# Gate and up products of 18 features as seven half-size block products

## The chip, the core and the metric

One core of a Trainium2 chip runs the whole program. The metric is the time of one execution in device microseconds (us), the median of several runs. The engines are TensorE (PE in the profile; its weight loads PEld), VectorE (DVE), ScalarE (ACT), GpSimd (POOL) and SyncE (SP, which issues the DMAs). Each works through its own instructions in program order and waits on counting semaphores.

## The reference

Two layers on 512 tokens of width 1024, float32, each with a feed-forward (FFN), a token mixer, and a second feed-forward; then a last norm.

```python
def swiglu(h, w_gate, w_up, w_down):
    return (jax.nn.silu(h @ w_gate) * (h @ w_up)) @ w_down

for l in range(DEPTH):                      # DEPTH = 2, D_MODEL = 1024, D_FF = 2816, SEQ = 512
    x = x + 0.5 * swiglu(rmsnorm(x, ffn1_norm[l]), ffn1_w_gate[l], ffn1_w_up[l], ffn1_w_down[l])
    ...                                     # x = x + [ssd || hgrn2](rmsnorm(x) @ w_in[l]) @ w_out[l]
    x = x + 0.5 * swiglu(rmsnorm(x, ffn2_norm[l]), ffn2_w_gate[l], ffn2_w_up[l], ffn2_w_down[l])
return rmsnorm(x, final_norm)
```

The change touches the four feed-forwards only; the mixers stay as they are.

## The kernel before

Everything lies with channels on the 128 partitions and the 512 tokens along the free side. x is 8 tiles of 128x512 that stay in SBUF. A float32 product is made of three matmuls of type float32r: each operand is split in a high part (a copy rounded to float32r, by ScalarE) and a low part (operand minus high part), and `products` adds high x high, high x low and low x high in PSUM (lines 1467 to 1469).

Weights come in **blocks** of 128x1024 floats (eight 128x128 tiles). There are four buffers each for the raw block (`raw`), its high part (`whi`) and its low part (`wlo`), and block w uses buffer w mod 4. For every block SyncE issues a DMA when the low part of block w-4 is made (`split`), ScalarE copies raw to `whi` when the products of block w-4 are done (`blk`; `hi`, `hi_i`), and GpSimd subtracts to make `wlo` (L481, semaphore `high` to `split`). TensorE waits for `split`.

A feed-forward (`ffn(c, wb, ...)` exists once for each engine; c is 0 or 1) has 44 gate and up blocks, two for each of 22 features of 128 (a "feature" here is a tile of 128 hidden units, gate block first). The first four blocks are interleaved (`up_staggered`: steps 0 to 10, block q takes the input tile k = step - q), since the input tiles `hhi`, `hlo` arrive one by one. The norm's factor per token is not in them: TensorE turns the sums of squares (`norm_turns`, after step 6), VectorE makes the reciprocal root, TensorE spreads it (`norm_spreads`, after step 8), and VectorE keeps it in `r`. Each gate and up product leaves PSUM through VectorE times `r` (L962, L964). Then ScalarE applies silu (L551), VectorE multiplies (L967), ScalarE copies the high part to `ahi` (L555), and VectorE makes the low part `alo` (L969). `ahi` and `alo` hold all 22 features.

The down product follows: for each of the 8 output tiles m, 22 x 3 matmuls over three blocks, and VectorE adds half of it to x (L985); ScalarE and VectorE make the next stage's `hhi` and `hlo` (L506, L848) and the sum of squares (L498, L858).

The order of the work is the order in which these functions are written, one program for each engine; there is no scheduler.

## Time and profile before

| | us |
|---|---|
| median of 3 runs | 1927.21 (1926.32 to 1927.46) |
| span of the profiled execution | 1927.2 |
| TensorE busy | 1919.3 |
| VectorE, ScalarE, GpSimd busy | 754.3, 701.8, 904.0 |

A row of a group of instructions gives line, engine, operation, output<-inputs, shape and count, then the busy time, the mean of one in ns, and the idle time of the engine just before them with what ended it. Matmuls overlap, so their spacing (from start to start) tells what one costs, not the duration in the row.

### The profile page before, as it was taken

To read this page: it belongs to the slowest core of one execution; us is meant where nothing else is said; L and a number is where in the kernel's file an instruction comes from. 1 tells how busy PE (TensorE), PEld (TensorE's weight loads), DVE (VectorE), ACT (ScalarE), POOL (GpSimd) and SP (SyncE) were. 2 spreads that over 40 slices of the span, in tenths; PEclk is the share of its full clock that TensorE was granted. 3 is DMA by queue.
4 is the path that set the end of the run, shared out by engine and by line. 5 is a ranking of instruction groups with operands and counts; after the bars stand their busy time and mean duration, and the time that the engine had idled before them with its cause. 6 is when DMAs were issued, how large, how long until landed. Compare 5 with 4: busy or idle time off the path is not lost.

```text
span 1927.2 us, 28344 instructions
## 1 busy us (share of the span) xinstructions
PE 1919.3 (100%) x10396; PEld 1579.1 (82%) x10396; DVE 754.3 (39%) x1209; ACT 701.8 (36%) x975; POOL 904.0 (47%) x550
## 2 busy tenths in 40 slices
PE   9999999999999999999999999999999999999999
PEld 7888888788788888888888888887878888888887
DVE  6222221389875322231132222214898752222312
ACT  5222222365643322222332222324556432222223
POOL 3444444466335544444444444444654444444443
PEclk9999999999999999999999999999999999999999
DMA  5332333322213333333323333332222223333332
GB/s 182 104 99 90 96 97 99 99 67 89 67 55 99 109 98 98 97 90 100 103 93 98 99 91 93 97 100 89 78 79 75 66 91 108 98 98 95 91 100 97
DMA packets 53504, 181.84 MB, mean 94 GB/s; under 512 B 6816, under 2 KB 6816, under 8 KB 53408
## 3 DMA queue, kind: packets, MB, share of 16 engines
q1 hardware_dynamic: 53264, 180.56, 30.1%
q8 instruction: 60, 0.98, 0.2%
q14 instruction: 36, 0.29, 0.1%
q10 hardware_dynamic: 144, 0.00, 0.0%
HBM read 178.45 MB, written 2.10 MB: 94 GB/s over the span
## 4 chain that ended last, share of the span: by engine, by line
PE 99%; DMA 0%; ACT 0%; DVE 0%; issue 0%; SPq 0%; ACTq 0%
PE ps L1467 31%; PE ps L1469 31%; PE ps L1468 31%; PE ps L1685 1%; PE ps L1602 1%; PE ps L1604 1%; PE ps L1603 1%; PE ps L1733 0%; PE ps L1799 0%; PE ps L1963 0%; PE ps L1746 0%; PE ps L1804 0%; DMA x<-in_x 0%; PE ps L1487 0%; PE ps L1783 0%; PE ps L1717 0%
## 5 line engine op out<-in xcount | busy, mean ns | idle before, releaser
L481 POOL TENSOR_TENSOR wlo<-raw,whi 128x1024 fp32r<-128x1024 f32 (+1 forms) x536 | 901.7, 1698 | 1015.2 <-ACT whi L542 553.6
L1467 PE MATMUL ps<-hhi,whi 128*128 128x512 f32 x1760 | 691.6, 393 | 2.2 <-DVE hlo L848 1.7
L1469 PE MATMUL ps<-hhi,wlo 128*128 128x512 f32 x1760 | 686.5, 390 | 0.0
L1468 PE MATMUL ps<-hlo,whi 128*128 128x512 f32 x1760 | 686.3, 390 | 0.0
L1467 PEld LDWEIGHTS ps<-hhi,whi 128*128 128x128 f32 x1760 | 330.9, 188 | 76.1 <-issue 4.1
L1469 PEld LDWEIGHTS ps<-hhi,wlo 128*128 128x128 f32 x1760 | 330.9, 188 | 69.6
L1468 PEld LDWEIGHTS ps<-hlo,whi 128*128 128x128 f32 x1760 | 331.0, 188 | 67.4
L1469 PE MATMUL ps<-ahi,wlo 128*128 128x512 f32 x704 | 274.1, 389 | 0.0
L1467 PE MATMUL ps<-ahi,whi 128*128 128x512 f32 x704 | 274.1, 389 | 0.0
L1468 PE MATMUL ps<-alo,whi 128*128 128x512 f32 x704 | 274.1, 389 | 0.0
L536 ACT ACTIVATE whi<-raw 128x1024 fp32r<-128x1024 f32 x168 | 177.2, 1055 | 265.3 <-PE ps L1469 246.0
L964 DVE TENSOR_TENSOR u<-ps,r 128x512 f32<-128x512 f32 x88 | 60.8, 691 | 368.5 <-PE ps L1469 368.5
L542 ACT ACTIVATE whi<-raw 128x1024 fp32r<-128x1024 f32 x176 | 183.5, 1045 | 38.9 <-PE ps L1469 38.9
L555 ACT ACTIVATE ahi<-u 128x512 f32 (+1 forms) x88 | 55.6, 632 | 389.1 <-DVE u L967 389.1
L985 DVE SCALAR_TENSOR_TENSOR x<-ps,x 128x512 f32<-128x512 f32 x32 | 22.1, 692 | 368.7 <-PE ps L1469 368.7
L1467 PEld LDWEIGHTS ps<-ahi,whi 128*128 128x128 f32 x704 | 132.2, 188 | 27.5
L1468 PEld LDWEIGHTS ps<-alo,whi 128*128 128x128 f32 x704 | 132.2, 188 | 27.4
L1469 PEld LDWEIGHTS ps<-ahi,wlo 128*128 128x128 f32 x704 | 132.2, 188 | 27.2
L551 ACT ACTIVATE g<-g 128x512 f32<-128x512 f32 x88 | 55.6, 631 | 237.9 <-DVE g L962 237.9
L962 DVE TENSOR_TENSOR g<-ps,r 128x512 f32<-128x512 f32 x88 | 60.8, 691 | 167.6 <-PE ps L1469 166.7
L969 DVE TENSOR_TENSOR alo<-u,ahi 128x512 f32 x88 | 66.1, 751 | 81.7 <-ACT ahi L555 81.7
L506 ACT ACTIVATE hhi<-x,par 128x512 fp32r<-128x512 f32 x48 | 34.6, 721 | 152.5 <-DVE x L985 132.8
(276 smaller groups left out, 1354.6 us busy)
## 6 DMA issues: line engine op xcount, KB each, us to landing
raw<-in_up SPq DMA_DIRECT2D x168, 512.0 KB, 3.4
raw<-in_mix SPq DMA_DIRECT2D x64, 512.0 KB, 3.4
raw<-in_dn SPq DMA_DIRECT2D x64, 448.0 KB, 3.3
raw<-in_dn SPq DMA_DIRECT2D x32, 512.0 KB, 3.5
raw<-in_lead SPq DMA_DIRECT2D x8, 512.0 KB, 3.5
x<-in_x SPq DMA_DIRECT2D x8, 256.0 KB, 6.2
raw<-in_lead SPq DMA_DIRECT2D x8, 256.0 KB, 6.3
raw<-in_mix SPq DMA_DIRECT2D x8, 256.0 KB, 2.5
```

The costliest lines, as they stand in the source:

```text
L481: low = pool.tensor_tensor(wlo[:, q, part], raw[:, q, part], whi[:, q, part].bitcast(F32), ALU.subtract)
L506: act.activation(hhi[:, m, :], x[:, m, :], ACT.Copy, scale=gain).then_inc(x_high.sem, 1)
L536: act.activation(whi[:, q, :], raw[:, q, :], ACT.Copy).then_inc(high.sem, 1)
L542: act.activation(whi[:, q, :], raw[:, q, :], ACT.Copy).then_inc(high.sem, 1)
L551: act.activation(g2[:, jj, :], g2[:, jj, :], ACT.Silu).then_inc(silu_g.sem, 1)
L555: act.activation(ahi[:, 2 * i + jj, :], u2[:, jj, :], ACT.Copy).then_inc(hid_high.sem, 1)
L962: made(g_out, tt(g2[:, jj, :], bank(jj), r[:], ALU.mult))
L964: made(u_out, tt(u2[:, jj, :], bank(2 + jj), r[:], ALU.mult))
L969: made(hid_low, tt(alo[:, 2 * i + jj, :], u2[:, jj, :], ahi[:, 2 * i + jj, :].bitcast(F32), ALU.subtract))
L1467: mm(dst, whi[:, q, s], mh, start=start, stop=False)
L1468: mm(dst, whi[:, q, s], ml, start=False, stop=False)
L1469: return mm(dst, wlo[:, q, s], mh, start=False, stop=stop)
```

## The change

It applies to features 4 to 21 of each feed-forward; features 0 to 3 (`PLAIN`) stay as before. Such a feature is a **unit**. Its two blocks, gate and up, are each cut in the halves k = 0 to 3 and 4 to 7 of the input channels: A11, A12 (gate) and A21, A22 (up), each 128x512. The tokens are cut in two halves of 256 (`HT`). The seven products of Strassen's scheme in Winograd's form are A11 B11, S1 T1, S2 T2, S4 B22, S3 T3, A12 B21 and A22 T4, each of 4 x 3 matmuls with 256 columns (`half_product`). The weight sums S1 = A21 + A22, S2 = S1 - A11, S4 = A12 - S2 are made by VectorE in PSUM (`make_sum`), S3 = A11 - A21 by GpSimd in SBUF (`make_s3`). ScalarE copies the high part of each of the seven to a slot of `whi` (`slot_hi`), and the low parts are made by VectorE (the three sums, `slot_low`) and GpSimd (A11, S3, A12, A22).

The token side has seven terms for each of four channel pairs k, 7 x 256 = 1792 columns: B11, B21, B22 and T1 to T4. `make_terms(k)` (VectorE) makes them from x, the norm's gain and `r`, so the norm is already in them; ScalarE copies the high part (`terms_hi`), and the low part is made by VectorE for k = 0, 1 and by GpSimd for k = 2, 3 (`terms_low`). All four must be there before the first unit.

Partial results are summed in PSUM as far as the scheme lets them; ScalarE copies three intermediate banks to SBUF (`copy_first`, `copy_second`, `copy_third`), VectorE adds them (`gate_second`, `up_second`, `gate_first`). A unit is finished before the next one ends its own products.

The features are worked in two parts, 0 to 11 and 12 to 21, each followed by a down product over its features (two blocks for each of 8 output tiles); the first adds to x at once (`x_part`). So the hidden tiles need less room, and the terms get it. From the second feed-forward on, the norm's turn and spread stand after steps 3 and 5 of the interleaved blocks; in the very first they stay after 6 and 8. All loops over features are now written out.

```diff
@@ -34,8 +34,43 @@
-DN_PIECES = [(0, 8), (8, 15), (15, 22)]
-DN_BLOCKS = KD * len(DN_PIECES)
+
+
+PLAIN = 4
+UNITS = NJ - PLAIN
+PARTS = [(0, 12), (12, NJ)]
+PIECES = [[(0, 6), (6, 12)], [(12, 17), (17, 22)]]
+HT = T // 2
+KH = KD // 2
+HW = KH * P
+
+
+T1, T3, T2, T4, B21, B22, B11, B12 = range(8)
+TERMS = 7
+MOVES = (B11, T1, T2, B22, T3, B21, T4)
+A11, S1, S2, S4, S3, A12, A22 = range(7)
+
...
+        def slot(weights, i):
+
+            return weights[:, i // 2, i % 2 * HW:i % 2 * HW + HW]
+
+        def quarter(b, k):
+
+            return raw[:, b % NS, k * HW:k * HW + HW]
+
...
+                def terms_low(k):
+                    pool.wait_ge(terms_high.sem, terms_high.upto(l, KH * c + k))
+                    pool.tensor_tensor(tlo[c][:, k, :], terms[c][k % 2][:, 0:TERMS, :].rearrange("p i t -> p (i t)"),
+                                       thi[c][:, k, :].bitcast(F32), ALU.subtract).then_inc(terms_low_pool.sem, 1)
...
+                def prepare(u):
+                    low_a11(u)
+                    make_s3(u)
+                    low_s3(u)
+                    low_a12(u)
+
+                for b in range(NS, 2 * PLAIN):
+                    low(l, wb + b)
+                    if b >= 2 * PLAIN - 2:
+                        terms_low(b - 2 * PLAIN + KH)
+                for part, (j0, j1) in enumerate(PARTS):
+                    u0 = max(j0, PLAIN)
+                    prepare(u0)
+                    for u in range(u0, j1):
+                        low_a22(u)
+                        if u + 1 < j1:
+                            prepare(u + 1)
+                    for m in range(KD):
+                        for i, (k0, k1) in enumerate(PIECES[part]):
+                            low(l, wb + down_block(part, m, i), (k1 - k0) * P)
...
+                    def terms_hi(k):
+                        act.wait_ge(terms_made.sem, terms_made.upto(l, KH * c + k))
+                        act.activation(thi[c][:, k, :], terms[c][k % 2][:, 0:TERMS, :].rearrange("p i t -> p (i t)"),
+                                       ACT.Copy).then_inc(terms_high.sem, 1)
...
+                    terms_hi(0)
+                    hi(wb + 4)
+                    plain_silu(0)
+                    hi(wb + 5)
+                    terms_hi(1)
+                    plain_silu(1)
+                    hi(wb + 6)
+                    hi(wb + 7)
+                    hidden_hi(0)
+                    terms_hi(2)
+                    hidden_hi(1)
+                    terms_hi(3)
+                    plain_silu(2)
+                    slot_hi(PLAIN, A11)
+                    hidden_hi(2)
+                    slot_hi(PLAIN, S1)
+                    slot_hi(PLAIN, S2)
+                    slot_hi(PLAIN, S4)
+                    plain_silu(3)
+                    slot_hi(PLAIN, S3)
+                    slot_hi(PLAIN, A12)
+                    hidden_hi(3)
...
+                    def make_terms(k):
+                        t = terms[c][k % 2]
+                        if k >= 2:
+                            ready(terms_low_dve, 2 * c + k - 2)
+                        did(stt(t[:, B21:B22 + 1, :].rearrange("p i t -> p (i t)"), x[:, KH + k, :], gain(KH + k), r[:],
+                                ALU.mult, ALU.mult))
+                        did(stt(t[:, B11:B12 + 1, :].rearrange("p i t -> p (i t)"), x[:, k, :], gain(k), r[:],
+                                ALU.mult, ALU.mult))
+                        settle()
+                        did(tt(t[:, T1, :], t[:, B12, :], t[:, B11, :], ALU.subtract))
+                        did(tt(t[:, T3, :], t[:, B22, :], t[:, B12, :], ALU.subtract))
+                        settle()
+                        did(tt(t[:, T2, :], t[:, B22, :], t[:, T1, :], ALU.subtract))
+                        settle()
+                        made(terms_made, tt(t[:, T4, :], t[:, B21, :], t[:, T2, :], ALU.subtract))
+
+                    def terms_low(k):
+                        ready(terms_high, KH * c + k)
+                        made(terms_low_dve, tt(tlo[c][:, k, :],
+                                               terms[c][k % 2][:, 0:TERMS, :].rearrange("p i t -> p (i t)"),
+                                               thi[c][:, k, :].bitcast(F32), ALU.subtract))
...
+                    def make_sum(u, n):
+
+                        b, v = wb + up_block(u), index(u)
+                        dst = bank(sum_bank(u, n))
+                        if n == 2 or u > PLAIN:
+                            ready(slot_low_dve, 3 * v + n - 2)
+                        if u == PARTS[1][0] + 1 and n == 0:
+                            ready(x_part, KD * c + KD - 1)
+                        if n == 0:
+                            loaded_block(b + 1)
+                            ins = tt(dst, quarter(b + 1, 0), quarter(b + 1, 1), ALU.add)
+                        elif n == 1:
+                            loaded_block(b)
+                            ready(sum_made, 3 * v)
+                            ins = tt(dst, bank(sum_bank(u, 0)), quarter(b, 0), ALU.subtract)
+                        else:
+                            ready(sum_made, 3 * v + 1)
+                            ins = tt(dst, quarter(b, 1), bank(sum_bank(u, 1)), ALU.subtract)
+                        made(sum_made, ins)
+
+                    def slot_low(u, n):
+                        i = (S1, S2, S4)[n]
+                        ready(slot_high, 5 * index(u) + i)
+                        made(slot_low_dve, tt(slot(wlo, i), bank(sum_bank(u, n)), slot(whi, i).bitcast(F32),
+                                              ALU.subtract))
...
+                    def up_second(u):
+                        ready(unit_done, 5 * index(u) + S3)
+                        ready(unit_copied, 3 * index(u) + 1)
+                        made(unit_out, tt(upper(u)[1][:, HT:T], bank(unit_banks(u)[0])[:, 0:HT], sq[:, HT:T], ALU.add))
+
...
+                    for part, (j0, j1) in enumerate(PARTS):
+                        u0 = max(j0, PLAIN)
+                        for u in range(u0, j1):
+                            more = u + 1 < j1
+                            if u > u0:
+                                hidden_first(u - 1)
+                            if more:
+                                make_sum(u + 1, 0)
+                                make_sum(u + 1, 1)
+                            if u > u0:
+                                hidden_lo(u - 1)
+                            if more:
+                                slot_low(u + 1, 0)
+                                make_sum(u + 1, 2)
+                                slot_low(u + 1, 1)
+                            gate_second(u)
+                            if more:
+                                slot_low(u + 1, 2)
+                            up_second(u)
+                            gate_first(u)
+                            hidden_second(u)
+                        hidden_first(j1 - 1)
+                        hidden_lo(j1 - 1)
+                        if part == 0:
+                            u = PARTS[1][0]
...
+                        return products(bank(2 * (q % 2) + q // 2), q, k, h_tile(k, c), k == 0, k == KD - 1)
+
+                    turns_at, spreads_at = (KD - 2, KD) if (l, c) == (0, 0) else (3, 5)
...
+                    def half_product(u, i, dst, start):
+
+                        cols = slice(MOVES[i] * HT, MOVES[i] * HT + HT)
+                        wh, wl = slot(whi, i), slot(wlo, i)
+                        for k in range(KH):
+                            s = slice(k * P, k * P + P)
+                            mm(bank(dst)[:, 0:HT], wh[:, s], thi[c][:, k, cols], start=start and k == 0, stop=False,
+                               skip_group_check=True)
+                            mm(bank(dst)[:, 0:HT], wh[:, s], tlo[c][:, k, cols], start=False, stop=False,
+                               skip_group_check=True)
+                            last = mm(bank(dst)[:, 0:HT], wl[:, s], thi[c][:, k, cols], start=False, stop=k == KH - 1,
+                                      skip_group_check=True)
+                        last.then_inc((unit_done if i < A12 else blk).sem, 1)
+
+                    def unit(u):
+
+                        q, z, y = unit_banks(u)
+                        v, b = index(u), wb + up_block(u)
+                        ready(slot_low_pool, 2 * v)
+                        if u == PLAIN:
+                            ready(terms_low_dve, 2 * c + 1)
+                            ready(terms_low_pool, 2 * c + 1)
+                        if u < PLAIN + 2:
+                            ready(g_out, PLAIN * c + PLAIN - 1)
+                            ready(u_out, PLAIN * c + PLAIN - 1)
+                        else:
+                            ready(hid, NJ * c + u - 2)
+                        half_product(u, A11, q, True)
+                        ready(slot_low_dve, 3 * v)
+                        if u >= PLAIN + 2:
+                            ready(unit_out, 3 * (v - 2))
+                        half_product(u, S1, z, True)
+                        ready(slot_low_dve, 3 * v + 1)
+                        ready(unit_copied, 3 * v)
+                        half_product(u, S2, q, False)
+                        ready(slot_low_dve, 3 * v + 2)
+                        ready(unit_copied, 3 * v + 1)
+                        half_product(u, S4, z, False)
+                        ready(slot_low_pool, 2 * v + 1)
+                        ready(unit_copied, 3 * v + 2)
+                        half_product(u, S3, q, False)
+                        ready(split, b)
+                        if u >= PLAIN + 2:
+                            ready(unit_out, 3 * (v - 2) + 2)
+                        half_product(u, A12, y, True)
+                        ready(split, b + 1)
+                        ready(unit_out, 3 * v + 1)
+                        half_product(u, A22, q, False)
+
```

**First place: ScalarE at the start of a feed-forward.** Before, with `whi<-raw` the copies of weight blocks, `g<-g` the silu:

```order
L541 ISA [waits raw_full0]
L542 ACT_TABLE_LOAD
L542 ACTIVATE whi<-raw 128x1024 [waits blk]
L550 ISA
L551 ACT_TABLE_LOAD
L551 ACTIVATE g<-g 128x512 [waits g_out]
```

and now, with `thi` the high part of the terms:

```order
L720 ACTIVATE thi_65<-terms_0_61 128x1792 [waits terms_made]
L705 ISA
L711 ISA [waits raw_full0]
L712 ACTIVATE whi<-raw 128x1024 [waits blk]
L727 REGISTER_ALU
L724 ACT_TABLE_LOAD
L724 ACTIVATE g<-g 128x512 [waits g_out]
```

The copy of block 4 stood first and needed only its data; now the high part of terms(0), which needs `r`, stands ahead of it.

**Second place: GpSimd in the first feed-forward's plain phase.** Before, with one subtraction for each weight block:

```order
L481 TENSOR_TENSOR wlo<-raw,whi 128x1024 [waits high]
L478 REGISTER_ALU
L481 TENSOR_TENSOR wlo<-raw,whi 128x1024 [waits high]
L478 REGISTER_ALU
L481 TENSOR_TENSOR wlo<-raw,whi 128x1024 [waits high]
```

and now, from block 5 on (block 4's stands ahead of these):

```order
L586 TENSOR_TENSOR wlo<-raw,whi 128x1024 [waits high] x2
L595 TENSOR_TENSOR tlo_67<-terms_0_61,thi_65 128x1792 [waits terms_high]
L586 TENSOR_TENSOR wlo<-raw,whi 128x1024 [waits high]
L595 TENSOR_TENSOR tlo_67<-terms_1_62,thi_65 128x1792 [waits terms_high]
L599 TENSOR_TENSOR wlo<-raw,whi 128x512 [waits slot_high]
L612 TENSOR_TENSOR s_69<-raw 128x512 [waits raw_full1,raw_full0]
```

Two term lows of 1792 columns (`tlo`) have moved in, the first between the weight blocks 6 and 7, the second behind block 7; then come the first unit's A11 and S3.

**Third place: VectorE in a feature.** Before, one of the two features of the loop's body:

```order
L962 TENSOR_TENSOR g<-ps,r 128x512 [waits blk]
L963 ISA
L964 TENSOR_TENSOR u<-ps,r 128x512 [waits blk]
L965 ISA
L966 ISA [waits u_out]
L967 TENSOR_TENSOR u<-g,u 128x512 [waits silu_g]
L969 ISA [waits hid_high]
L969 TENSOR_TENSOR alo<-u,ahi 128x512
```

and now, from the middle of a steady unit u (`wlo<-ps,whi` is a slot low of unit u+1, `ps<-raw,ps` its third sum, the 256-column rows gate_second, up_second and gate_first of unit u):

```order
L1338 TENSOR_TENSOR wlo<-ps,whi 128x512 [waits slot_high]
L1233 REGISTER_ALU [waits slot_low_dve]
L1332 TENSOR_TENSOR ps<-raw,ps 128x512 [waits sum_made]
L1233 REGISTER_ALU
L1338 TENSOR_TENSOR wlo<-ps,whi 128x512 [waits slot_high]
L1347 TENSOR_TENSOR g<-ps,acc 128x256 [waits unit_copied,unit_done]
L1233 REGISTER_ALU
L1338 TENSOR_TENSOR wlo<-ps,whi 128x512 [waits slot_high]
L1233 REGISTER_ALU
L1357 TENSOR_TENSOR u<-ps,sq 128x256 [waits unit_copied,unit_done]
L1233 REGISTER_ALU
L1352 TENSOR_TENSOR g<-ps,sq 128x256 [waits unit_copied,blk]
```

`up_second` (`u<-ps,sq`), for which TensorE waits ahead of the product A22, stands behind all three slot lows of the next unit, and each of these waits for a copy by ScalarE.

## Rows read from the trace of the kernel before

**Rows 1.** The page's part 1: busy time, share and instructions of each engine.
```profile
PE 1919.3 (100%) x10396; PEld 1579.1 (82%) x10396; DVE 754.3 (39%) x1209; ACT 701.8 (36%) x975; POOL 904.0 (47%) x550
```

**Rows 2.** The page's part 4: the chain that ended last, by engine.
```profile
PE 99%; DMA 0%; ACT 0%; DVE 0%; issue 0%; SPq 0%; ACTq 0%
```

**Rows 3.** Busy time by stretch, of gate and up work: us, engines (count), clock, DMA.
```profile
40.00:280.00 240.00, 240.00 (x1061) 198.78 (x1060) 62.57 (x94) 69.71 (x87) 111.17 (x47) 1.00 0.32 100
```

**Rows 4.** Timeline of TensorE near the start: start, duration, what, idle before.
```profile
8.64 0.65 PE L1467 MATMUL ps<-hhi,whi 128*128 128x512 f32 x1 [1.68 <-DVE hlo L848]
9.08 0.63 PE L1468 MATMUL ps<-hlo,whi 128*128 128x512 f32 x1
...
12.39 0.40 PE L1467 MATMUL ps<-hhi,whi 128*128 128x512 f32 x1
12.62 0.40 PE L1468 MATMUL ps<-hlo,whi 128*128 128x512 f32 x1
```

**Rows 5.** Timeline of the output's turn, weight loads and matmuls.
```profile
1918.16 4.77 PEld L1963 LDWEIGHTS ps<-g,x 128*128 128x128 f32 x42
1918.19 4.93 PE L1963 MATMUL ps<-g,x 128*128 128x128 f32 x42
```

**Rows 6.** The page's part 5: groups of instructions, busy us, mean ns, idle before.
```profile
L985 DVE SCALAR_TENSOR_TENSOR x<-ps,x 128x512 f32<-128x512 f32 x32 | 22.1, 692 | 368.7 <-PE ps L1469 368.7
L969 DVE TENSOR_TENSOR alo<-u,ahi 128x512 f32 x88 | 66.1, 751 | 81.7 <-ACT ahi L555 81.7
L551 ACT ACTIVATE g<-g 128x512 f32<-128x512 f32 x88 | 55.6, 631 | 237.9 <-DVE g L962 237.9
L542 ACT ACTIVATE whi<-raw 128x1024 fp32r<-128x1024 f32 x176 | 183.5, 1045 | 38.9 <-PE ps L1469 38.9
```

**Rows 7.** Timeline of VectorE and GpSimd before the second feed-forward.
```profile
603.38 2.39 POOL L481 TENSOR_TENSOR wlo<-raw,whi 128x1024 fp32r<-128x1024 f32 x1 [2.27 <-ACT whi L536]
...
603.95 2.38 DVE L848 SCALAR_TENSOR_TENSOR hlo<-x,par,hhi 128x512 fp32r<-128x512 f32 x1 [1.01 <-ACT hhi L506]
606.25 0.68 DVE L858 TENSOR_TENSOR acc<-acc,sq 128x512 f32<-128x512 f32 x1
```

**Rows 8.** Three lines' instructions: duration ns, min/median/max.
```profile
L848 DVE SCALAR_TENSOR_TENSOR hlo<-x,par,hhi x48: 751/752/2818, 266.9 to 1917.1; 128x512 fp32r<-128x512 f32 x48
...
L1155 DVE TENSOR_TENSOR w<-e,f x32: 412/897/964, 416.8 to 1430.1; 128x256 f32<-128x256 f32 x32
...
L481 POOL TENSOR_TENSOR wlo<-raw,whi x536: 723/2384/2875, 27.2 to 1918.1; 128x1024 fp32r<-128x1024 f32 x93, 128x256 fp32r<-128x256 f32 x86
```

**Rows 9.** Timeline of the helpers in one feature of the loop.
```profile
109.87 0.69 DVE L967 TENSOR_TENSOR u<-g,u 128x512 f32<-128x512 f32 x1 [0.17 <-DVE u L964]
110.69 0.63 ACT L555 ACTIVATE ahi<-u 128x512 f32 x1 [4.82 <-DVE u L967]
111.23 1.04 ACT L542 ACTIVATE whi<-raw 128x1024 fp32r<-128x1024 f32 x1
111.49 0.69 DVE L969 TENSOR_TENSOR alo<-u,ahi 128x512 f32 x1 [0.93 <-ACT ahi L555]
112.35 2.39 POOL L481 TENSOR_TENSOR wlo<-raw,whi 128x1024 fp32r<-128x1024 f32 x1 [4.00 <-ACT whi L542]
```

**Rows 10.** Timeline of the norm in the first and second feed-forward.
```profile
30.54 0.69 DVE L871 COPY r<-ps 128x512 f32<-128x512 f32 x1 [2.09 <-PE ps L1487]
...
617.01 0.60 PE L1481 MATMUL ps<-ident,acc 128*128 128x128 f32 x4
...
620.39 0.16 DVE L834 SCALAR_TENSOR_TENSOR rt<-ps,rt 128x4 f32<-128x4 f32 x1
```

**Rows 11.** The page's part 6: DMA issues, KB each, us to landing.
```profile
raw<-in_up SPq DMA_DIRECT2D x168, 512.0 KB, 3.4
```

**Rows 12.** ScalarE's 512-column copies out of PSUM, by form: busy us, mean ns.
```profile
L578 ACT ACTIVATE b<-ps 128x512 f32<-128x512 f32 x8 | 4.7, 588 | 0.0
```

493 lines of the change are left out of this document (380 added, 113 removed).

## Prediction

> **What bounds the kernel now.** I read the page's engine row first: TensorE is busy for 1919.3 of 1927.2 us, VectorE 754, ScalarE 702, GpSimd 904 [rows 1]. The chain that ended last lies on TensorE for 99% [rows 2], and in a stretch of feed-forward work TensorE has 1061 matmuls in 240.00 us without a gap, 226.2 ns each, at the full clock (2.4 GHz) [rows 3]. So the time is the number of matmuls times 226.2 ns, and every helper engine has slack. The change takes matmul columns away and gives the helpers more to do, so two questions decide: what a matmul of 256 columns costs, and whether VectorE, ScalarE and GpSimd still keep ahead. Only TensorE's start is bare, with 1.68 us of waiting, after which the clock fell to 1.2 GHz: eight starts lie 0.43 us apart, then 0.23 again [rows 4].
>
> **Part 1, the matmuls removed.** A feature now takes 2 blocks x 8 x 3 = 48 matmuls of 512 columns, 48 x 0.2262 = 10.86 us. A Strassen unit takes 7 products x 4 x 3 = 84 matmuls of 256 columns. No row has this form. The nearest is the output turn L1963: each streams 106.7 ns (128 f32 columns at two cycles each), with a full 128-column weight load: 42 starts in (4.93 - 0.28)/41 = 0.113 us [rows 5]. A fixed extra per matmul (226.2 - 213.3 = 12.9 ns) would have made that 119.6, so I take half of 226.2, 113.1 ns. Bounds: 112 ns (the loads' own spacing, (4.77 - 0.19)/41 [rows 5]) and 119.6 ns. Unit: 84 x 0.1131 = 9.50 us, saving 1.36 us; 4 feed-forwards x 18 = 72 units: **-98 us**, between -105 and -58 us. The down products have the same count, cut at feature 12, each piece 5 or 6 features instead of 7 or 8, with 8 more updates of x per feed-forward of 0.69 us [rows 6]; TensorE needs 8.1 us for such a product, so they hide.
>
> The Trainium skill ("TensorE: Matmul & The Clock Gate", section Back-to-back issue gap) gives 262 cycles (109 ns) for 256 columns and 518 (216 ns) for 512; the trace has 226 ns for the latter, so it does not agree. By the page's figure the removal would be 72 x (10.86 - 84 x 0.109) = 123 us.
>
> **Part 2, the port that VectorE and GpSimd share.** A VectorE instruction with two SBUF inputs that begins during a GpSimd instruction finishes only 0.55 us after that one: GpSimd runs 603.38 to 605.77 and hlo, 0.75 us otherwise, from 603.95 to 606.33 [rows 7]; L848's longest is 2.82 us and its shortest 0.75, and GpSimd's 1024-column instruction has 2.38 median and 2.88 at worst [rows 8]. So they exclude each other. The skill's "SBUF — State Buffer" page, section Who interferes with whom, calls this an exclusive lock held for the whole instruction; the trace agrees, and without it the forecast would be the faster rival below. Durations: VectorE 512 columns 0.69 and 256 columns 0.41 [rows 6, 8], so 1792 columns 0.69 + 1280 x 0.0011 = 2.1; GpSimd 256 columns 0.72 and 1024 2.39 [rows 8, 9], so 512 columns 1.28 and 1792 4.05; ScalarE 512 columns 0.63, 1024 1.05 [rows 6, 9], so 1792 1.7; a PSUM source 0.59 [rows 12]. Handover between engines takes 0.03 to 0.17 us beyond the end of an instruction [rows 9].
>
> **Part 3, the plain phase of a feed-forward** (features 0 to 3, making the seven token terms). Take the second one. Before, the norm's turn (step 6, after 22 x 3 matmuls) stands at 617.01, so the phase began at 602.1; x_sum is ready at 606.93 [rows 7, 10], in time for the new turn at step 3 (608.9). The norm chain takes 620.39 + 0.16 - 617.01 = 3.5 us, the spread at step 5 is at 614.9 and r is copied by about 616.2. TensorE ends blocks 0 to 3 at 625.0 and would end 4 to 7 at 646.7. Until the first unit may begin VectorE has, in its program order: four make_terms of 3.2 us (2 x 0.75 + 4 x 0.42), two lows of 2.1, eight evacuations, three hidden and three lows, three sums and three slot lows, 30.6 us. Waits for ScalarE's copies in between (1.2 and 0.6 behind the terms, 0.8 for each hidden or slot copy) add 7.2: 37.8, so 654.0 at the earliest, a stall of 7.3 us. GpSimd owns the port in the same time for 4 x 2.39 + 2 x 4.05 + 1.28 = 18.9 us; met in full it is 672.9, a stall of 26.2. Followed row by row: terms(0) 619.4; ScalarE's copy of it 621.1, of block 4 622.1; GpSimd waits out VectorE's low until 623.2, block 4 is ready at 625.5 (stall 0.6). VectorE's two first instructions of terms(1) meet GpSimd's lows of blocks 4 and 5 (2.3 and 2.9 us for 0.75 each), so terms(1) is ready at 630.6; its low ends 634.4; hidden(0) meets block 6 (2.9 us), ending 637.2; low(0) 638.6; terms(2) ready at 641.6, copied 643.4. Only now can GpSimd do terms_low(2), to 647.5, and **block 7's low is queued behind it** (second order excerpt of the change): ready at 650.4, where TensorE wanted it at 641.9 to 642.4: stall 8.1. Meanwhile hidden_lo(1) waits for that terms_low (4.1 us), the first stt of terms(3) for block 7's low (2.9), terms(3) is ready 653.3, hidden(2) waits for terms_low(3) until 659.7, then sums and slot lows go one by one through ScalarE to 666.2, and the evacuation of feature 3 lets unit 4 begin at 667.6, where TensorE is free at 657.2: stall 10.4. Total 19 us, three times (the last about 18). In the **first** feed-forward the turn stays at steps 6 and 8, r is there at 31.2 [rows 10], and ScalarE's copy of block 4, at once ready before, now stands behind terms_hi(0) (first excerpt): 31.2 + 3.2 + 1.7 + 1.1, then 2.39 behind a low on the port, 40.8, where TensorE is free at 32.5: stall 8.1, and then 6.4 and 10.1: 24.6. Sum: **+81 us**, between +32 and +111.
>
> **Part 4, the steady unit.** In 9.50 us VectorE does three sums and three slot lows, one hidden low (7 x 0.61 back to back) and five of 256 columns (5 x 0.35): 6.1 us. Waits of its order: 0.3 behind its own sums, 0.8 until ScalarE copied the second sum, 0.9 until silu: 8.1. Three of its instructions have two SBUF inputs (sum 0, hidden_lo, hidden_second), each may wait for one of GpSimd's five of 1.28: up to 11.9. The wait that ends last is TensorE's before product A22 for up_second, which stands behind the third slot low (third excerpt). Following the order through two units gives 20.04, so 10.0 for one: +0.5, less in the units behind a long stall: 72 x 0.44 = **+32 us**, between 0 and 72 x 2.4. ScalarE (9 x 0.54 + 3 x 0.30, some 5.8 us) has slack. Raw blocks land 3.4 us after issue [rows 11] and are asked for a unit ahead.
>
> **Part 5, the clock.** Each of the two long stalls per feed-forward (6 to 10 us) is longer than the one of 1.68 us that cost eight matmuls 0.2 us each [rows 4]: 8 x 1.6 = **+13 us**, between 0 and 26. Restarts with a bare weight load (0.19 us [rows 5]) beyond those in the walk: **+2**.
>
> **Sum.** The profiled execution's span of 1927.2 is also the median of the runs. -98 + 81 + 32 + 13 + 2 = +30: **1957 us**.
>
> **Rivals.** *Faster: the helpers miss each other on the port.* Instructions that meet GpSimd in the walk in fact fall between its own; plain phases cost 7.3 x 3 and 13, units nothing, clock 0 to 4: -98 + 35 + 2 = 1866, and with half of the port's waits about 1912. For it: VectorE's 88 hidden lows met little before (0.69 alone [rows 9], mean 0.75 [rows 6]). Against: GpSimd's load rises from 4.8 in 10.9 to 6.4 in 9.5 us per feature. *The fixed extra per matmul:* 119.6 ns; -58, while units of 10.05 us hide their chain: +81 + 13 + 9 = 1972. *Much slower: every meeting is met.* Plain phases 26.2 x 3 + 32 = 111, units 1.0 more each, 72, clock 15: 2027; it decides from an order in which GpSimd's instructions begin just ahead of VectorE's. *The change doesn't do what it says:* a 256-column matmul bound by its weight load at 129 ns or more would save nothing; rows 5 speak against it, with 112.
>
> **Chances.** Forecast (1932 to 1990) 0.47, fixed extra 0.13, helpers miss each other 0.24, much slower 0.13, no saving per unit 0.03. A measurement tells 0.2% (3.9 us) from no change. Faster: 0.24, plus little from the forecast's lower edge: 0.25. Within: 0.04. Slower: 0.71. The range leaves out half of the faster rival and most of the much slower one: 1895 to 2005.
>
> **What would show it.** Spacing of the 256-column matmuls near 113 ns (112 to 114: part 1; near 120: the second rival). TensorE waits before block 7 for GpSimd and before unit 4's first product for VectorE, 8 and 10 us, and waits for the turn of none. Two-input VectorE instructions that last 1 to 4 us. TensorE's wait before A22 in every second unit, about 0.7 us, released by VectorE. Granted clock below 1 after each long wait. I am wrong if the plain phases show under 10 us of idle each, or if the clock falls inside the steady units.

## The result and the profile after

The changed kernel takes **1993.64 us** (median of 4 runs, 1992.51 to 1995.6) where the kernel before takes 1926.94 (1926.32 to 1927.46): a ratio of 1.0346, 95% interval 1.0331 to 1.0361. It is 66.7 us slower; the forecast was 30 slower. The profiled execution has a span of 1993.8 us.

The page of the changed kernel, its engine row and its chain, as [rows 1, 2] of before:

```profile
PE 1899.4 (95%) x12988; PEld 1679.1 (84%) x12988; DVE 1270.6 (64%) x1924; ACT 951.5 (48%) x1599; POOL 1074.6 (54%) x806
...
PE 85%; DVE 8%; issue 5%; ACT 2%; DVEq 0%; ACTq 0%
```

TensorE was busy all the time; now it waits for 5% of it, and the chain runs through VectorE, ScalarE and "issue". The view of the waits tells for whom TensorE waits (us in total, times, longest):

```profile
PE ps L1935 <- POOL wlo L586: 38.4, 8, 8.0
PE ps L2042 <- DVE u L1299: 36.7, 4, 9.6
PE ps L2210 <- issue: 8.1, 3, 3.2
PE ps L2242 <- issue: 1.8, 1, 1.8
```

The first two are the plain phases: weight blocks late by GpSimd, and unit 4 by VectorE's evacuation of feature 3. The last two aren't in a feed-forward at all. L2210 and L2242 are the small matmuls of the mixer, which the change doesn't touch.

Next, where the time is, stage by stage. I cut the spacing of TensorE's large matmuls in both traces in three parts: what they cost at the full clock (226.4 ns for 512 columns, 119.9 for 256), what lies above that up to the spacing at 1.2 GHz ("half clock"), and waiting. Each entry is before and after, in us.

| stage | time | matmuls | waiting | half clock |
|---|---|---|---|---|
| first feed-forward | 368.7, 385.5 | 359.2, 344.7 | 1.8, 25.9 | 2.1, 9.2 |
| first mixer | 230.8, 239.2 | 184.5, 184.5 | 0, 0.7 | 3.7, 5.5 |
| second feed-forward | 361.5, 372.1 | 360.5, 346.1 | 0, 20.7 | 0.3, 4.6 |
| third | 360.2, 371.3 | 359.2, 344.6 | 0, 19.9 | 0.4, 6.1 |
| second mixer | 230.9, 240.1 | 184.5, 184.6 | 0, 0.9 | 3.7, 6.4 |
| fourth | 361.5, 371.9 | 360.5, 346.1 | 0, 20.7 | 0.3, 4.5 |

In the feed-forwards the removal is worth 57.9 us (14.5 each), the waiting costs 85.4, the half clock 21.3. The mixers are 8.4 and 9.2 us longer, nearly all of it in their small matmuls, which this table leaves out, and in the half clock behind them. -57.9 + 85.4 + 21.3 + 17.6 = +66.4. The last two columns are cut by the spacing alone and not by the clock. In the mixers of before the granted clock is 1.00, so their 3.7 us are no half clock, and only the differences count there. In the feed-forwards now, some 3 us of the half clock are short waits at the full clock; taken from the stretches whose granted clock is below 1, the four have some 20 us where they had 2.

**What a matmul of 256 columns costs.** Timeline of TensorE in unit 4 of the second feed-forward (start, duration, what):

```profile
699.77 0.28 PE L2044 MATMUL ps<-tlo,whi 128*128 128x256 f32 x1
699.89 0.28 PE L2046 MATMUL ps<-thi,wlo 128*128 128x256 f32 x1
700.01 0.28 PE L2042 MATMUL ps<-thi,whi 128*128 128x256 f32 x1
700.13 0.28 PE L2044 MATMUL ps<-tlo,whi 128*128 128x256 f32 x1
```

They start 0.12 us apart, at the full clock, not 0.113.

**The port.** Timeline of VectorE and then of GpSimd while the terms of pair 1 are made; it answers to [rows 7, 8]:

```profile
648.85 2.29 DVE L1275 SCALAR_TENSOR_TENSOR terms<-x,par,r 128x512 f32<-128x512 f32 x1
651.07 2.89 DVE L1277 SCALAR_TENSOR_TENSOR terms<-x,par,r 128x512 f32<-128x512 f32 x1
653.99 0.42 DVE L1280 TENSOR_TENSOR terms<-terms 128x256 f32<-128x256 f32 x1
...
647.30 6.11 POOL L586 TENSOR_TENSOR wlo<-raw,whi 128x1024 fp32r<-128x1024 f32 x2 [16.26 <-ACT whi L712]
```

The two instructions that take 0.75 us alone take 2.29 and 2.89 beside two GpSimd lows, which themselves take 6.11 instead of 4.8. I had forecast 2.3 and 2.9. The worst meeting comes later, 4.10 us for 0.69, with GpSimd's low of terms 3 from 679.94 to 683.97:

```profile
680.42 4.10 DVE L1304 TENSOR_TENSOR u<-g,u 128x512 f32<-128x512 f32 x1 [0.49 <-ACT g L724]
```

**The mixer's gap.** Timeline of TensorE in a burst of small matmuls of the first mixer, where the kernel before had no gap:

```profile
447.28 1.01 PE L2210 MATMUL ps<-w 64*32 64x32 f32 x43
450.47 0.33 PE L2210 MATMUL ps<-w 64*64 64x64 f32 x3 [2.19 <-issue]
```

"issue" means that no wait and no engine released it. There are two such gaps in each mixer, of 2.2 and 2.7 us, 1.8 and 3.2, and behind each the clock stands at half for 3.41 us. The row of the first one in the busy time by stretch, with the clock as the third value from the end:

```profile
450.88:454.29 3.41, 3.41 (x19) 2.74 (x20) 3.34 (x10) 0.00 (x0) 0.00 (x0) 0.51 0.47 159
```

### The profile page after: what moved, and what is told of

It reads as the page before. It is cut to its first block, busy times and chain, and to the rows that moved or that the text cites. A ratio compares the mean times of both kernels' runs of the same rounds, so it can differ in the third digit from the quotient of the medians.

```text
span 1993.8 us, 36545 instructions
## 1 busy us (share of the span) xinstructions
PE 1899.4 (95%) x12988; PEld 1679.1 (84%) x12988; DVE 1270.6 (64%) x1924; ACT 951.5 (48%) x1599; POOL 1074.6 (54%) x806
## 4 chain that ended last, share of the span: by engine, by line
PE 85%; DVE 8%; issue 5%; ACT 2%; DVEq 0%; ACTq 0%
PE ps L1935 15%; PE ps L1936 15%; PE ps L1937 15%; PE ps L2042 12%; PE ps L2044 11%; PE ps L2046 11%; DVE u L1304 1%; DVE terms L1275 1%; DVE terms L1277 1%; PE ps L2210 1%; PE ps L2127 1%; PE ps L2129 1%; PE ps L2128 1%; ACT thi L720 1%; ACT whi L764 1%
## 5 line engine op out<-in xcount | busy, mean ns | idle before, releaser
L2042 PE MATMUL ps<-thi,whi 128*128 128x256 f32 x2016 | 578.6, 287 | 39.4 <-DVE u L1299 36.7
L2044 PE MATMUL ps<-tlo,whi 128*128 128x256 f32 x2016 | 573.9, 285 | 0.0
L2046 PE MATMUL ps<-thi,wlo 128*128 128x256 f32 x2016 | 573.6, 285 | 0.0
L586 POOL TENSOR_TENSOR wlo<-raw,whi 128x768 fp32r<-128x768 f32 (+2 forms) x168 | 322.8, 1929 | 368.3 <-ACT whi L712 319.1
L2042 PEld LDWEIGHTS ps<-thi,whi 128*128 128x128 f32 x2016 | 389.9, 193 | 46.5 <-issue 45.8
L2044 PEld LDWEIGHTS ps<-tlo,whi 128*128 128x128 f32 x2016 | 390.3, 194 | 0.2
L2046 PEld LDWEIGHTS ps<-thi,wlo 128*128 128x128 f32 x2016 | 389.9, 193 | 0.0
L1935 PE MATMUL ps<-hhi,whi 128*128 128x512 f32 x608 | 250.9, 413 | 39.1 <-POOL wlo L586 38.4
L1936 PE MATMUL ps<-hlo,whi 128*128 128x512 f32 x608 | 244.1, 401 | 0.3 <-issue 0.3
L1937 PE MATMUL ps<-hhi,wlo 128*128 128x512 f32 x608 | 243.7, 401 | 0.0
```

The source lines that it names most:

```text
L586: pool.tensor_tensor(wlo[:, q, 0:width], raw[:, q, 0:width], whi[:, q, 0:width].bitcast(F32), ALU.subtract).then_inc(split.sem, 1)
L1935: mm(dst, whi[:, q, s], mh, start=start, stop=False)
L1936: mm(dst, whi[:, q, s], ml, start=False, stop=False)
L1937: return mm(dst, wlo[:, q, s], mh, start=False, stop=stop)
L2042: mm(bank(dst)[:, 0:HT], wh[:, s], thi[c][:, k, cols], start=start and k == 0, stop=False, skip_group_check=True)
L2044: mm(bank(dst)[:, 0:HT], wh[:, s], tlo[c][:, k, cols], start=False, stop=False, skip_group_check=True)
```

## The experiments

They ask in turn what a short matmul costs, what the port and the queue order have to do with the waits, what the half clock costs, where the mixer's gaps come from, and whether the scheme can pay at all.

### Columns cut in two with the same weights

```diff
-                        return products(bank(2 * (q % 2) + q // 2), q, k, h_tile(k), k == 0, k == KD - 1)
+                        edge = 256 if c == 0 else 384
+                        for w, moving in ((whi, mh), (whi, ml), (wlo, mh)):
+                            for cut in (slice(0, edge), slice(edge, T)):
+                                last = mm(dst[:, cut], w[:, q, s], moving[:, cut],
+                                          start=k == 0 and w is whi and moving is mh,
+                                          stop=k == KD - 1 and w is wlo, skip_group_check=True)
```

> The kernel before with each gate and up matmul of 512 columns cut in two with the same weights, each with its own weight load: 256 and 256 in the first feed-forward of each layer, 384 and 128 in the second. Nothing else changes. Fixed extra per matmul (12.9 ns beside 0.4167 ns a column): spacings of 119.6 ns for 256 columns and 172.9 for 384; a matmul of 128 columns would be 66 and is held at the 112 ns of a weight load. That adds 1056 x 13 ns = 14 us to each first and 1056 x (173 + 112 - 226) ns = 62 us to each second feed-forward: about 2079 us. Cost in proportion to the columns: 113.1 and 169.7 ns, 0 and 59 us: about 2044 us. If it is the weight load that holds the 256-column matmul at 120 ns, the 384-column one is at 170, not 173, and the 128-column one at 120: about 2087 us.

Measured: 2085.98 us (one run). Spacing of the 256-column matmuls 120 ns; a pair of 384 and 128 columns takes 287 ns. Two rows of the second feed-forward, five pairs apart, (701.27 - 699.84)/5 = 0.286 us:

```profile
699.84 0.45 PE L1534 MATMUL ps<-hhi,wlo 128*128 128x384 f32 x2
...
701.27 0.39 PE L1534 MATMUL ps<-hlo,whi 128*128 128x384 f32 x1
```

(Two accumulations are open in one bank at a time here, and their sums aren't the reference's; only the times are read.) So the 120 ns belongs to the form and isn't made by the changed kernel. The pair is nearer to 173 + 112 = 285 ns than to 170 + 120 = 290. The time is nearer to the third figure (2087) than to the first (2079), but TensorE has three gaps by "issue" in the second mixer of this run, 3.3 us in all, that none of the theories has. So this run favours the fixed extra and doesn't settle it.

### One width at a time

```diff
+                        n = {(0, 0): 384, (0, 1): 320, (1, 0): 256, (1, 1): 192}[l, c]
+                        n0 = T if k == 0 else n
+                        mm(dst[:, 0:n0], whi[:, q, s], mh[:, 0:n0], start=k == 0, stop=False, skip_group_check=True)
+                        mm(dst[:, 0:n], whi[:, q, s], ml[:, 0:n], start=False, stop=False, skip_group_check=True)
+                        return mm(dst[:, 0:n], wlo[:, q, s], mh[:, 0:n], start=False, stop=k == KD - 1,
+                                  skip_group_check=True)
```

> The kernel before; in each gate and up product the matmuls take the first 384, 320, 256 or 192 token columns only (first to fourth feed-forward; the very first matmul of a product still takes 512). The other columns' products are left out, so the output is not the reference's. No second matmul with the same weights follows, so each width stands alone. Fixed extra per matmul (12.9 ns beside 0.4167 ns a column): 172.9, 146.2, 119.6 ns, and 92.9 or, if a weight load takes longer than that, its time, near 117 to 120. A weight load that holds every short matmul at 120 ns and no fixed extra: 169.7, 141.4, 120 and 120. Cost in proportion to the columns: 169.7, 141.4, 113.1, 113.

Measured: 1587.82 us (one run); what counts is the spacing. Timelines of TensorE in the first, second and fourth feed-forward (first and last of 9, 9 and 8 rows in a row):

```profile
99.72 0.33 PE L1535 MATMUL ps<-hhi,wlo 128*128 128x384 f32 x1
...
101.11 0.33 PE L1534 MATMUL ps<-hlo,whi 128*128 128x384 f32 x1
...
639.80 0.31 PE L1533 MATMUL ps<-hhi,whi 128*128 128x320 f32 x1
...
640.98 0.31 PE L1535 MATMUL ps<-hhi,wlo 128*128 128x320 f32 x1
...
1399.78 0.27 PE L1534 MATMUL ps<-hlo,whi 128*128 128x192 f32 x1
...
1400.57 0.27 PE L1535 MATMUL ps<-hhi,wlo 128*128 128x192 f32 x1
```

(101.11 - 99.72)/8 = 0.174 us, (640.98 - 639.80)/8 = 0.147, (1400.57 - 1399.78)/7 = 0.113. Medians over whole products, with what the columns alone take at 0.4167 ns each:

| columns | spacing, ns | columns alone | extra |
|---|---|---|---|
| 512 | 226.2 | 213.3 | 12.9 |
| 384 | 173.8 | 160.0 | 13.8 |
| 320 | 146.8 | 133.3 | 13.5 |
| 256 | 119.9 | 106.7 | 13.2 |
| 192 | 110.6 | 80.0 | 30.6 |

At the full clock the extra is fixed, 13 to 14 ns a matmul, down to 256 columns. Below that something else holds the spacing, near 111 ns: the load of 128 weight columns. A row of the kernel before shows that it is the load. These matmuls stream one column each, and their eight loads still lie (0.97 - 0.19)/7 = 0.111 us apart:

```profile
1917.27 0.97 PEld L1474 LDWEIGHTS ps<-ones,acc 128*128 128x128 f32 x8
```

At the half clock there is no extra. In the changed kernel, behind the wait before unit 4, matmuls of 256 columns lie 0.213 us apart, which is 256 columns at 1.2 GHz and nothing more, and those of 512 lie 0.427 apart:

```profile
694.40 0.41 PE L2042 MATMUL ps<-thi,whi 128*128 128x256 f32 x1
694.61 0.41 PE L2044 MATMUL ps<-tlo,whi 128*128 128x256 f32 x1
694.83 0.41 PE L2046 MATMUL ps<-thi,wlo 128*128 128x256 f32 x1
```

### Block 7's low ahead of the terms low

```diff
                 for b in range(NS, 2 * PLAIN):
                     low(l, wb + b)
-                    if b >= 2 * PLAIN - 2:
-                        terms_low(b - 2 * PLAIN + KH)
+                terms_low(2)
+                terms_low(3)
```

> The changed kernel with GpSimd's low part of weight block 7 ahead of its low part of terms 2 (the two terms lows stand together behind it). Theory of the prediction, each queued wait costs its own time: the 8 us waits before block 7 go and the wait before unit 4 stays near 9.5: 1993.6 - 5.6 - 3 x 8 - 4 us of clock = 1960 us. Rival, the sum of work on the shared port and on VectorE sets when unit 4 can begin, and the queue order only says where TensorE waits for it: the waits before block 7 go, those before unit 4 become 17 to 19 us, 1988 to 1993 us.

Measured: 1987.14 us (one run), 6.5 less than the changed kernel. Waits of TensorE:

```profile
PE ps L2042 <- DVE u L1299: 72.5, 4, 18.7
PE ps L1935 <- POOL wlo L586: 9.6, 4, 8.0
```

The waits before block 7 are gone, as both theories said, and the four before unit 4 have grown from 36.7 to 72.5 us, to 18.7 at the longest. The queue order of one engine decided only where TensorE waits for the plain phase.

### GpSimd's lows in short pieces

```diff
+            def low_pieces(l, w):
+                q = w % NS
+                pool.wait_ge(high.sem, high.upto(l, w))
+                for i in range(4):
+                    cut = slice(i * 256, i * 256 + 256)
+                    last = pool.tensor_tensor(wlo[:, q, cut], raw[:, q, cut], whi[:, q, cut].bitcast(F32),
+                                              ALU.subtract)
+                last.then_inc(split.sem, 1)
...
                 for b in range(NS, 2 * PLAIN):
-                    low(l, wb + b)
+                    low_pieces(l, wb + b)
```

and the same for the terms lows, seven pieces.

> The changed kernel with GpSimd's lows of the plain phase cut in pieces of 256 columns (four for a weight block, seven for a term pair); the amount of work is the same and GpSimd has 3 x 4 + 6 x 2 = 24 instructions more for each feed-forward. Theory, the port is held for a whole instruction and passes between the engines at its end: VectorE's two-input instructions wait 0.8 us instead of up to 2.9 or 4.6, the long waits before block 7 shrink a little and those before unit 4 mostly go: about 1963 us. Rival, the engines share the port by amount of work, or the lows themselves are on TensorE's path: GpSimd is slower by 24 x 0.17 = 4 us for each feed-forward, 1993 to 2005 us.

Measured: 1964.59 us (1963.29 to 1965.24), ratio to before 1.0189, interval 1.0172 to 1.0206. That is 29 us less than the changed kernel, with more instructions and 35 us more of GpSimd's busy time. TensorE's waits, and the duration of VectorE's first instruction of a term pair (ns, shortest, median, longest), which is L1275 in the changed kernel and L1287 here:

```profile
PE ps L1947 <- POOL wlo L594: 46.0, 8, 9.3
PE ps L2054 <- DVE u L1311: 3.5, 4, 0.9
```

```profile
L1287 DVE SCALAR_TENSOR_TENSOR terms<-x,par,r x8: 741/984/1228, 634.3 to 1626.9; 128x512 f32<-128x512 f32 x8
```

and in the changed kernel:

```profile
L1275 DVE SCALAR_TENSOR_TENSOR terms<-x,par,r x8: 745/1516/2823, 641.4 to 1656.5; 128x512 f32<-128x512 f32 x8
```

The longest falls from 2.82 to 1.23 us: the port passes at the end of an instruction, and how long one holds it is how long the other may wait. In exchange VectorE meets GpSimd more often: the four 256-column instructions of a term pair, 0.42 us each in the changed kernel, have medians of 0.63 to 0.68 us here. The Trainium skill's page "SBUF — State Buffer" (Who interferes with whom) calls the shared pair of ports an exclusive lock, and the trace agrees. Block 7 still waits, because it still stands behind a terms low.

### Another order on three engines

The edit is only the order of the calls of the plain phase. The start of VectorE's, before and after:

```diff
 make_terms(0)
-plain_gate(0)
-terms_low(0)
-plain_up(0)
 make_terms(1)
+plain_gate(0)
 plain_gate(1)
+terms_low(0)
+plain_up(0)
 plain_up(1)
-terms_low(1)
 plain_hidden(0)
-hidden_lo(0)
 make_terms(2)
```

> The changed kernel with nothing but another order in the plain phase, on three engines. VectorE: make_terms(0), make_terms(1), then gate and up of features 0 and 1, terms(2) and (3) ahead of most hidden lows, the sums of unit 4 between features 2 and 3. ScalarE: the block copies 4 to 7 ahead of the silus. GpSimd: all four block lows, then the two terms lows. The steady units are as they were. Theory, the waits come from meetings on the port and from instructions that stand behind a partner's late result, so an order that lets each engine's next input be ready takes off most of them: about 9 of the 25 us of waiting and half clock are left in each feed-forward, 1941 us. Rival, the sum of helper work bounds the phase, as the run with block 7's low moved up says (it gained 6.5 us): 1980 to 1990 us.

Measured: 1941.95 us (1941.08 to 1942.26), ratio to before 1.0072, interval 1.0056 to 1.0087. Waits of TensorE:

```profile
PE ps L2048 <- POOL wlo L599: 28.9, 4, 7.6
PE ps L1941 <- POOL wlo L586: 7.2, 1, 7.2
```

Of 75 us of waits in the plain phases 36 are left, and 52 us of time are gone, with the same instructions but for a few waits among VectorE's own. So the rival that pool7 had spoken for, that the sum of work bounds the phase, is wrong too: moving one engine's work moved the wait, moving three engines' work together removed half of it.

### TensorE kept busy in its waits

```diff
+                    def keep_busy(n):
+                        for _ in range(n):
+                            mm(bank(7), hhi[c][:, 0, 0:P], hhi[c][:, 0, :], start=True, stop=True)
...
+                        if b == 7:
+                            keep_busy(22 if (l, c) == (0, 0) else 30)
...
+                        if u == PLAIN:
+                            keep_busy(34)
```

> The changed kernel with TensorE kept at work in its long waits of the plain phase: matmuls of 128x512 into a bank that nobody reads, 30 before block 7 (22 in the very first feed-forward, and 32 before its block 4) and 34 before unit 4, so 5 to 7.7 us of work in waits of 5.6 to 9.8 us; 20 tiny ones make the number of TensorE instructions ahead of each mixer a multiple of 256 larger, so that the gaps there stay. Theory, the clock falls because TensorE stood still: all nine stretches of half clock behind those waits go, and with them 9.2 + 4.6 + 6.1 + 4.5 = 24 us (the clock column of my sums by stage), and the restarts: 1968 to 1970 us. Theory of the size on record, 1.6 us for each of eight waits: 1980 us. Rival, work in the waits costs the helpers nothing but the waits were longer than needed for them: same, 1993 us.

Measured: 1992.62 us (1990.31 to 1997.57), ratio to before 1.0336, interval 1.0318 to 1.0355. The median is 1 us below the changed kernel's, which is within what the runs scatter; the expectation's 1980 and 1968 to 1970 us are ruled out. Yet half of the half clock is gone: by the same reckoning as in the table the four feed-forwards have 3.1, 2.9, 3.9 and 2.9 us of it instead of 9.2, 4.6, 6.1 and 4.5, so 12.8 instead of 24.4 (by the granted clock some 7 instead of 20). Busy time of this kernel by stretch, block 7 and what follows in the second feed-forward, and the same block in the changed kernel:

```profile
673.30:686.20 12.90, 12.90 (x58) 10.58 (x57) 10.82 (x14) 3.97 (x5) 7.46 (x3) 1.00 0.12 42
```

```profile
675.50:682.70 7.20, 7.20 (x24) 5.67 (x24) 6.61 (x10) 2.74 (x3) 2.76 (x1) 0.72 0.21 73
```

With the clock at 1.00 block 7 is done sooner, and TensorE waits that much longer for VectorE: unit 4 begins 66.6 us behind the start of that feed-forward here and 66.4 in the changed kernel. The half clock of block 7 was not on the path. The half clock behind the wait before unit 4 is on it, and most of it is left, since TensorE still waits 3.7 us there (1.0 in the very first feed-forward): the first unit took 11.6 us here and 12.0 there, and 10.07 at the full clock. What that part costs, this run doesn't test.

### up_second ahead of the third slot low

```diff
                             gate_second(u)
+                            up_second(u)
                             if more:
                                 slot_low(u + 1, 2)
-                            up_second(u)
```

> The changed kernel with VectorE's up_second(u) ahead of the third slot low of unit u+1. TensorE's wait before product A22 is 0.25 to 0.31 us in every second unit, some 34 of them in all. Theory: they go, and the later slot low still is ahead of the product S4 of the next unit, so the unit is bound by its 84 x 0.120 = 10.08 us: 1993.6 - 34 x 0.28 = 1984 us. Rival, the wait moves to another product of the unit (S4 for the third slot low, or the next A11 for hidden): 1993 us or more.

In the changed kernel such a wait is two starts that lie 0.41 us apart instead of 0.12:

```profile
712.85 0.28 PE L2046 MATMUL ps<-thi,wlo 128*128 128x256 f32 x1
713.26 0.35 PE L2042 MATMUL ps<-thi,whi 128*128 128x256 f32 x1
```

Measured: 1981.95 us (1976.76 to 1982.89), ratio to before 1.0280, interval 1.0262 to 1.0297: 11.7 us less than the changed kernel. The waits before A22 are gone from the trace and none took their place. Counted in the trace of the changed kernel they are 28, of 0.20 to 0.31 us, 7.1 us in all, and not 34. So they account for some 7 of the 11.7 us; where the rest comes from is not shown.

### TensorE's instructions moved by a whole block and by half a block

The four gaps in the mixers sit at records 5569, 6081, 19393 and 19905 of TensorE, counted from the start of the trace; the count takes in its loads and matmuls (2 x 12988) and the semaphore instructions between them, 26721 records in all. All four are 193 above a multiple of 256. And the page's DMA part has instruction transfers of 1.70 MB in 104 packets, 16 KB each, which is one for every 256 of those records. Before it was 0.98 MB in 60. The page of the changed kernel and, for comparison, that of the kernel whose TensorE was kept busy, which has 27361 records:

```profile
q8 instruction: 104, 1.70, 0.4%
```

```profile
q8 instruction: 107, 1.75, 0.3%
```

The eleven kernels with the scheme agree in this. The number of transfers (102 to 107) is in each exactly the number of records that stand 193 above a multiple of 256, and behind the first 20 us every idle time of TensorE over 0.15 us that the view puts down to "issue", long or short, stands at such a record. In the run with columns cut in two, which has another program, the three gaps are 512 records apart.

Two kernels put tiny matmuls in the wait before unit 4 of the first feed-forward, where they cost nothing:

```diff
+                        if (l, c, u) == (0, 0, PLAIN):
+                            for _ in range(64):
+                                mm(bank(6)[0:8, 0:8], ident[:, 0:8], ident[:, 0:8], start=True, stop=True)
```

> The changed kernel with 64 tiny matmuls (8 rows and columns out, 128 instructions with their weight loads) in TensorE's wait before unit 4 of the very first feed-forward, so that all TensorE instructions behind them stand 128 places later. The four new gaps inside the small mixer matmuls lie 512, 13824 and 512 TensorE records apart, all multiples of 256, and an instruction transfer of 16 KB (256 x 64 bytes) is under way at each. Theory, instruction supply: a gap needs a boundary of 256 instructions 60 to 105 places inside a burst of 376; after the shift the four boundaries lie outside that and the gaps of 2.3, 2.8, 1.9 and 3.3 us go, with the clock drop behind each, and one may appear in the fourth burst of the first mixer, which then has its boundary at place 95: 1979 to 1983 us. Rival, something the helper engines or the weight DMAs do: the gaps stay where they are, 1993 us.

Measured: 1995.27 us (1994.47 to 1995.63), ratio 1.0351, interval 1.0334 to 1.0368, and the gaps stood where they had been, at records 5825, 6337, 19649 and 20161. (The second and third gap are 13312 records apart, the second and fourth 13824.) By the words of the expectation that is the rival. But the records had moved by 256, not by 128: such a float32 matmul leaves four. A whole block of shift changes nothing in either theory, so the run told nothing apart, except that the new numbers are again 193 above a multiple of 256. Hence half as many, `range(32)`:

> The changed kernel with 32 tiny matmuls in TensorE's wait before unit 4 of the first feed-forward. In the run before, 64 of them left 256 more records of TensorE in the trace, not 128 (a float32 matmul leaves four), and 256 is a whole block; the gaps stayed, at records 5825, 6337, 19649 and 20161, which like those of the changed kernel (5569, 6081, 19393, 19905) are all 193 above a multiple of 256. Now the shift is half a block. Theory, instruction supply in blocks of 256: the gaps at places 320 to 358 of those bursts go, because the boundary now falls some 128 places earlier; 10.3 us of gaps and about 4 us of clock: 1979 us, or 1982 if the fourth burst of the first mixer, whose boundary comes to place 95 and 351, takes a gap instead. Rival, the small matmuls starve for another reason at that place of the program: the gaps stay, 1993 us.

Measured: 1981.88 us (1979.79 to 1982.65), ratio 1.0275, interval 1.0258 to 1.0293. The four gaps are gone, a new one of 1.5 us stands in the fourth burst of the first mixer, where there was none before, and a short one of 0.4 us in the first burst of the second. Timeline of the first:

```profile
495.76 0.67 PE L2213 MATMUL ps<-w 64*64 64x64 f32 x15
497.94 0.21 PE L2213 MATMUL ps<-w 64*64 64x64 f32 x1 [1.51 <-issue]
```

It is at record 7361, place 351 of its burst, the burst and the place that the expectation named. 64 tiny matmuls changed nothing and 32 took 12 us off: TensorE runs out of instructions where the end of a block falls in the wrong place of a burst.

### Six plain features

```diff
-PLAIN = 4
+PLAIN = 6
```

with the helpers' orders written for six, features 4 and 5 stored where terms 0 lay, and `up_second` ahead of the third slot low, `gate_second` ahead of the second. ScalarE's order inside the units is changed too. How much each of these is worth, no run tells apart.

> Six plain features in place of four (features 4 and 5 keep their hidden tiles where terms 0 lay), so that TensorE has 21.7 us more to do before the first unit; orders of the three helpers written for it, block lows of GpSimd ahead of the terms lows; up_second ahead of slot lows 1 and 2 in the units. 64 units are left, each 10.86 - 10.08 = 0.78 us less than a plain feature: 1928 - 50 = 1878 us, plus 4 us for the very first feed-forward, where r comes late, plus 1 us of wait before each first unit: 1885 us if TensorE waits for nothing else. Instruction supply: with the records that this kernel has, the boundaries fall to places 235, 208, 172 and 111 of the first mixer's four bursts and 49, 22, 242 and 181 of the second's; a gap is possible at 111 (the next boundary at 367, near the burst's end) and at 49, not elsewhere, 2 to 6 us with the clock: 1886 to 1891 us. Rival, the port stays the bound because the two features bring helper work of their own: waits of 5 to 8 us for each feed-forward, 1910 us or more.

Measured: 1897.26 us (1896.11 to 1900.46), ratio to before 0.9839, interval 0.9824 to 0.9854. It is the first kernel with the scheme that beats the one before, and 6 to 11 us above what was expected. A gap of 1.5 us stands at the end of the first mixer's fourth burst, as named (the boundary at 377, not 367; the view puts this one down to a weight block of GpSimd, though it stands at the record of a block's end), and two of 2.4 and 2.7 us in the second mixer's first and second, at places 335 and 308, of which I had named one: my count of the records was 10 to 30 off. The fourth feed-forward also has a wait of 2.1 us for GpSimd that the others lack.

> The same with TensorE's instruction blocks moved: the six warm-up matmuls of 192 columns at the very start are four of 256 (8 records less), and 9 tiny matmuls stand before block 4 of the second feed-forward (36 records more). The boundaries fall to places 243, 216, 180 and 119 in the first mixer (119 + 256 = 375, at the very end of the burst) and 21, 250, 214 and 153 in the second: no gap in either, 1882 to 1885 us, 1 to 6 us less than without the shift. If the shift does nothing, the two kernels have the same time and the same gaps.

Measured: 1892.15 us (1890.58 to 1893.98), ratio 0.9817, interval 0.9804 to 0.9831. Fewer gaps, but one of 2.7 us is left at place 307, for the same miscount. The last kernel moves that one:

```diff
-                        for _ in range(9):
+                        for _ in range(17):
                             mm(bank(7)[0:8, 0:8], ident[:, 0:8], ident[:, 0:8], start=True, stop=True)
```

> The kernel with six plain features and shifted instruction blocks, with 17 tiny matmuls in place of 9 before block 4 of the second feed-forward. Measured so far over all kernels: a gap comes where the second boundary of 256 records in a burst lies at places 307 to 358, none where it lies at 284 or below. The one gap left, 2.75 us at place 307 of the second mixer's first burst with 1.4 us of half clock behind it, has its boundary at place 275 now, and the other bursts of that mixer have none between 290 and 370. Theory: no gap in either mixer, 1892 - 4 = 1888 us. Rival: it stays or another one comes, 1892 us or more.

Measured: **1889.74 us** (1887.38 to 1891.53), ratio to before **0.9804**, interval 0.9789 to 0.9819. Of the gap of 2.7 us one of 0.3 is left, at place 275, and the granted clock no longer falls in a mixer. The difference to the run before, 2.4 us, is within what the two medians scatter; that the gap shrank is what its trace shows. Its page and TensorE's longest waits:

```profile
PE 1870.6 (99%) x12730; PEld 1646.6 (87%) x12730; DVE 1228.4 (65%) x1860; ACT 916.2 (49%) x1535; POOL 1061.7 (56%) x782
```

```profile
PE ps L2066 <- DVE u L1320: 4.2, 4, 1.6
PE ps L1959 <- POOL wlo L590: 2.5, 1, 2.5
PE ps L1959 <- DVE g L1314: 2.5, 1, 2.5
```

Before each first unit it waits for 0.9 to 1.6 us, where the changed kernel waited for 9, and otherwise for more than 0.5 us in the very first feed-forward only.

## Why the prediction was right or wrong

The direction held and the time is in the range (1895 to 2005); the size is more than twice the forecast. Of the 36.7 us between them part 1 makes +40, part 4 -24, part 3 -4, part 5 +8, the restarts -2 and the mixers, which had no term, +17.6. Parts 1 and 4 offset each other for the greater part, probably because one fault makes both; that the range held although the mixers were missing is partly luck. By its own steps:

- **Part 1, the matmuls removed: the step that failed most.** Forecast -98 us, measured -57.9. I had the fixed extra among the rivals, worked out right (119.6 ns, -58), and set it aside for [rows 5], the output's turn with 113 ns. The run with single widths and the row of L1474 show what bounds those rows: the load of 128 weight columns takes 111 to 113 ns, whether 1, 128 or 192 columns are streamed. They bound the spacing from below and say nothing of a longer stream of 256 columns. The argument with which I set the extra aside, that it would have made the turn 119.6 ns, doesn't carry over: the turn is of type float32 and the products are float32r, and why the one shows no extra while the other has 13 ns is open. The row that does speak is [rows 3], 226.2 ns for 512 columns at 0.4167 each: the 12.9 ns left over are no part of the columns and don't shrink with them. Of the Trainium skill's figures on "TensorE: Matmul & The Clock Gate" neither agrees: 109 ns for 256 columns in the section Back-to-back issue gap stands against 119.9 here, as 216 against 226.
- **Part 2, the port: right.** Durations forecast at 2.3, 2.9, 2.9 and 4.1 us came as 2.29, 2.89, 2.89 and 4.10. The run with pieces shows it as a cause, not just a row: 29 us from shorter instructions alone.
- **Part 3, the plain phase: right in size and place, and only half right in its reason.** Forecast 8.1 + 6.4 + 10.1 us in the first feed-forward, measured 8.1 + 5.6 + 9.2 (spacing above 0.226). In the others 0.6 + 8.1 + 10.4, measured 0.7 + 8.0 + 8.9 to 9.8. (The first 8.1 is a slip: 40.8 - 32.5 is 8.3.) Sum forecast 81, measured 77. But I had put the 8.1 us down to block 7's place in GpSimd's queue. With that mended alone, the time came back before unit 4, 18.7 us.
- **Part 4, the steady unit: wrong, for the most part by the fault of part 1.** Forecast 10.0 us with 9.50 of matmuls in it. Measured 20.53 for two, 10.27 each, with 84 x 0.120 = 10.08 of matmuls. The wait before A22 comes in every second unit, as said, but is 0.20 to 0.31 us, not 0.7; probably longer products leave the helpers more time, which no run tests. Where the sum had +32 above -98 there are -57.9 and some 8 us of waits outside the plain phases.
- **Part 5, the clock: too low as a row, too high as a cost.** Forecast 13 us, and the stages have 21.3 more of half clock (some 18 by the granted clock). But the kernel whose TensorE was kept busy has 1.0336 against 1.0346, intervals that overlap. I had added a term that lies for the most part beside other work: a slow block 7 makes TensorE late for a unit that isn't ready anyway. With 11.6 us of half clock taken away, 1 us came off the median. What the half clock in the first units costs is open. The rows of waits and of half clock in my table add up to the time, and still can't be saved one by one.
- **Not in the sum at all: the mixers, +17.6 us.** I had taken them as untouched, and their instructions are. The shift by half a block took 12 us of it away.
- **The restarts (2 us)** are too small to be told apart.

Of the rivals, the fixed extra came true, with 1972 us forecast: -58 + 81 + 13 + 9 there stand against -57.9, 77, 21.3 and 8 measured, and of the 22 us that it is short 17.6 are the mixers. "The helpers miss each other" and "every meeting is met" didn't come: the waits were those of the row-by-row walk. "Would show it" named 113 or near 120 ns as the test between forecast and rival, and it was 120.

Left open: what sets the width of the window in which a block's end makes a gap. Over the kernels built from the changed one there was a gap of 1.5 to 3.2 us with the second boundary of a burst at places 307 to 358, and one of 1.5 us at 377, which may be a wait for GpSimd. At 385, just behind the burst, it is 0.7 us or less, and at 284 and below there are only two, of 0.4 us (place 257) and 0.3 us (275); nothing between was tried. Also whether VectorE's waits by "issue" in the mixer (12.1 us in the changed kernel) are a cause or a consequence; TensorE's were gone without anything done to VectorE.

## What to carry to other kernels

Cost a shorter matmul as a fixed extra and a price per column, both from the longest form of the same type in the trace, and with the weight load as a floor; a row of another form tells only the one of these that binds it. Where several engines feed one phase, moving one engine's queue moves the wait; try the orders together, and give the phase more cover (two more plain features cost 1.6 us of matmuls in each feed-forward and, with the orders written for them, took its waiting from some 20 us to about 1) before giving up the scheme. Work that isn't touched can still change its time when the program ahead of it changes its length: look for idle time by "issue" in dense bursts of tiny instructions.

## What the runs showed of the hardware

- A float32r matmul with its own 128 x 128 weight load costs 13 to 14 ns and 0.4167 ns a column at the full clock, down to 256 columns; at 192 columns the load holds it at 110.6 ns, and with one column at 111. At the half clock the 13 ns are gone: 427 ns for 512 columns, 213 for 256. The Trainium skill's "TensorE: Matmul & The Clock Gate" (LDWEIGHTS) gives the load's time in ns as its columns divided by 1.2, by which an estimate for 128 is 107; the trace, with 111, is near it.
- TensorE's instructions come in transfers of 16 KB, a block of 256. In a burst of 376 tiny loads and matmuls, over within 2.5 us, the end of a block at an unlucky place leaves TensorE idle for 1.5 to 3.2 us, at the same instruction in every kernel whose program ahead of it differed by whole blocks. Moving the program by half a block with 32 tiny matmuls made the kernel 12 us faster, and by a whole block did nothing.
- The half clock after a wait costs little or nothing where the engine goes on to wait for something else: with 11.6 us of it taken away the medians differ by 1 us, within their scatter.
- VectorE and GpSimd pass the port at the end of an instruction: VectorE's longest wait fell with GpSimd's longest instruction, 2.82 to 1.23 us, and the kernel by 29 us.
